# Statistics of the memory's second rows moved behind two weight subtractions, with multiplications of ones on TensorE

## The chip, the cores and the metric

The kernel runs on one core of one Trainium2 chip, and the metric is the device time of one execution in microseconds. A core has TensorE (PE, with its weight loads shown as PEld), VectorE (DVE), ScalarE (ACT), GpSimd (POOL) and SyncE (SP), each with its own queue of instructions in program order, and 16 DMA engines.

## The reference

It computes two blocks of two layers on 256 positions of width 1024, in float32; the first block's result is the second's input. The first block has an even layer (differential attention, a short gated convolution, cross attention to a memory of 256 rows) and an odd one (forgetting attention and cross attention); the second has a gated linear recurrence with a convolution, a pooling mixer, two more cross attentions and two feed-forward parts. What the change touches is the first thing the kernel computes, the memory's keys and values of the even layer, and a scalar of the attention:

```
def rms_norm(x, g):
    y = xf * lax.rsqrt(jnp.mean(xf * xf, axis=-1, keepdims=True) + EPS)
    return (y * g.astype(jnp.float32)).astype(x.dtype)

# in memory_cross_attention
mk, mv = jnp.split(rms_norm(mem, mem_g) @ w_mem_kv, 2, axis=-1)

# in differential_attention
lam = jnp.exp(jnp.sum(lp[0] * lp[1])) - jnp.exp(jnp.sum(lp[2] * lp[3])) + lam_init
```

## The kernel before

Every product of a weight matrix is computed in three passes of fp32r matmuls: a float32 operand is split into a rounded half `hi` and the rest `lo`, and hi·hi, hi·lo and lo·hi are added up in a PSUM bank (`passes`, L550 to L555). Weights come in units of 1 MB, each in two halves of 512 KB, through two slots of `w_raw`. For each half SyncE issues the load (`load`, L393), ScalarE writes `w_hi` (`hi`, L1272), VectorE writes `w_lo = w_raw - w_hi` (`lo`, L1928, the instruction at L1932), and TensorE multiplies. SyncE waits with the load of a half until the subtraction that last read its slot is done. Units 0 and 1 (`e_kv`) have their loads issued without a wait; units 2 and 3 (`e_kv` too) follow in the same slots.

At the start the memory has to be turned. TensorE transposes the 256 x 1024 rows in 16 transposes into banks 6, 7, 2 and 3 (`turn_pairs`, L674, recorded as L685), ScalarE writes `y_hi` with the gain as scale (`turned_hi`, L1400, L1408), and VectorE writes `y_lo` (`turned_lo`, L2051, L2059), pair by pair. The factor of the norm isn't applied to the rows: it is a factor of each row of the product, so ScalarE applies it when it copies the product out of the bank (`scaled_out`, L1341). The statistics behind it are VectorE's: `tile_stats` (L1954, two instructions of 512 columns a tile), `row_stats` (L1958: aggregation at L1966, two small operations, then a request to POOL by `ask`), and POOL computes the power -0.5 (`power`, L1843, L1846).

The order on every engine is written out by hand. VectorE's begins at L2382: statistics of both tiles of the memory, the request, then in two steps two pairs of `y_lo` and one weight subtraction each (`lo(0, 0, 1)` and `lo(0, 1, 2)`), then the subtractions of unit 1 (`lo(1, half, ...)`), the statistics of x's first 128 rows (L2394), a wait for lambda's parameters (L2395), two products and a reduction on them (L2397 to L2400), the subtractions of unit 2, the statistics of x's second rows (L2406), the request for them, the normalisation of x, and the subtractions of unit 3. POOL's begins at L1838: three memsets, among them of `ones`, a wait for the request named "mem" and its power (L1849), then the loads of the forget bias (L1850) and of lambda's parameters (L1851, 128 KB to 128 partitions), then the next powers. ScalarE's begins at L1648, and it waits for the power of "mem" before it goes on to unit 2.

TensorE's begins at L1039: a transpose of the memory's gains, a wait for both tiles of the memory, the 16 transposes, a transpose of the next gains (L1046), then `row_of("e_kv", 0)` and `1`, each 24 matmuls in two halves that wait for their subtractions (`lo_done`), two transposes of gain rows, and `row_of("e_kv", 2)`. Behind that the normalised rows of x are turned (`turn_pairs(nrm, 2)`, eight transposes), followed by the first half of `row_of("e_kv", 3)`, the other eight transposes, and its second half. Bank 0 belongs to `e_kv` unit 0, whose first matmul clears it.

The two places in which POOL and VectorE stand in line with the load of lambda:

```
            power("mem")
            pool.dma_start(bc[0:12, :], t["o_c_forget_b"].rearrange("a h -> h a")).then_inc(bc_in, 16)
            pool.dma_start(tp[:, 0:256], t["e_a_lambda"].rearrange("l a b -> l (a b)").to_broadcast([P, 256])).then_inc(lam_in, 16)
...
            v.wait_ge(x_in[0], 16)
            tile_stats(hv, 0)
            v.wait_ge(lam_in, 16)
```

Of the kernel before, what the change touches and what calls it, by code (L numbers as in the profile page):

```python
# [26 lines left out]
P = 128  # L27
# [118 lines left out]
GCOL = {}  # L146
# [35 lines left out]
def turned(name, groups=None):  # L182

    return TURN_AT[name] + (dict(TURNS)[name] if groups is None else groups)
# [25 lines left out]
def build_program(nc, t, out):  # L210

    with ExitStack() as ctx:
        def sb(name, words, dt=F32):
            return ctx.enter_context(nc.sbuf_tensor(name, [P, words], dt))

        def sem(name):
            return ctx.enter_context(nc.semaphore(name))
# [18 lines left out]
        ones = sb("ones", P)  # L236
# [3 lines left out]
        bank = [ctx.enter_context(nc.psum_tensor(f"bank{i}", [P, 512], F32)) for i in range(8)]  # L240
# [21 lines left out]
        def two(ap, w):  # L262
            return ap.rearrange("p (m w) -> p m w", w=w)

        def tv(ap):
            return ap.rearrange("p (k n) -> p k n", n=SEQ)

        hv = two(h[:, :], D)
        uh, ul, yh_, yl_ = tv(u_hi), tv(u_lo), tv(y_hi[:, :]), tv(y_lo[:, :])
        nrm = two(att[:, 0:2 * D], D)  # L270
# [78 lines left out]
        mem_in, id_in = [sem("mem_in0"), sem("mem_in1")], sem("id_in")  # L349
# [4 lines left out]
        init_done = sem("init_done")  # L354
        pow_asked, pow_done = sem("pow_asked"), sem("pow_done")
        dve_step, act_step, pool_step = sem("dve_step"), sem("act_step"), sem("pool_step")
        gains_t, gains_ready = sem("gains_t"), sem("gains_ready")
# [191 lines left out]
        def _(pe):  # L549
            def passes(out_ap, pairs, start, stop_, last=False):  # L550

                (ah, al), (bh, bl) = pairs
                pe.matmul(out_ap, ah, bh, start=start, stop=False, skip_group_check=True)  # L553
                pe.matmul(out_ap, ah, bl, start=False, stop=False, skip_group_check=True)  # L554
                return pe.matmul(out_ap, al, bh, start=False, stop=stop_, skip_group_check=True)  # L555

            def keep_busy(bk, n):

                for _ in range(n):
                    pe.matmul(bank[bk][:, 0:SEQ], ident, cst[:, C_TRI:C_TRI + SEQ], start=True, stop=True)  # L560

            def k8_unit(slot, bk, xh, xl, wait_lo, wait_bank, fresh=None, between=None):

                for half in range(2):
                    if fresh is not None:
                        pe.wait_ge(tL, fresh[half])
                    if half == 1 and between is not None:
                        between()  # L570
                    pe.wait_ge(lo_done, wait_lo + half)
                    if half == 0 and wait_bank is not None:
                        pe.wait_ge(evacuated, wait_bank)
                    for m in range(2):
                        for k in range(4 * half, 4 * half + 4):
                            a = 2048 * slot + SEQ * k + P * m
                            mm = passes(bank[bk][:, SEQ * m:SEQ * m + SEQ],
                                        ((w_hi[:, a:a + P], w_lo[:, a:a + P]), (xh[:, k, :], xl[:, k, :])),
                                        half == 0 and m == 0 and k == 0, k == 7)
                    mm.then_inc(half_done, 1)  # L580
# [22 lines left out]
            def row_of(name, j, xh, xl, fresh=None, between=None):  # L603

                u, kb = UNIT0[name] + j, BANK0[name] + j - j % 2
                first = j - j % 2
                row_unit(u % 2, j % 2, (unit_bank(name, first), unit_bank(name, first + 1)), xh, xl, 2 * u + 1,
                         kb - 1 if kb else None, fresh, between)
# [14 lines left out]
            def k8_phase(name, xh, xl, n=None, skip=0):  # L623
                base, kb = UNIT0[name] + skip, BANK0[name] + skip
                n = COUNT[name] if n is None else n
                if n == 2:
                    for j in range(2):
                        k8_unit((base + j) % 2, (kb + j) % 2, xh, xl, 2 * (base + j) + 1, kb + j - 1)
                    return
                with pe.Fori(0, n // 2) as i:  # L630
                    for j in range(2):
                        k8_unit((base + j) % 2, (kb + j) % 2, xh, xl, 4 * i + (2 * (base + j) + 1), 2 * i + (kb + j - 1))
# [81 lines left out]
            def beside_norm(phase, name, xh, xl):  # L714

                for j in range(2):
                    u, kb = UNIT0[phase] + j, BANK0[phase] + j
                    k8_unit(u % 2, unit_bank(phase, j), xh, xl, 2 * u + 1, kb - 1,
                            between=(lambda: turn_normed(name, 0)) if j == 1 else None)
                turn_normed(name, 1)  # L720
# [318 lines left out]
            pe.wait_ge(id_in, 16)  # L1039
            pe.wait_ge(mrow_in, 16)  # L1040
            pe.transpose(bank[5][:, 0:8], rows[0:8, 0:P], ident[0:8, 0:8]).then_inc(gains_t, 1)
            for m in range(2):
                pe.wait_ge(mem_in[m], 16)
            turn_pairs(nrm, 4, (6, 7, 2, 3))
            pe.wait_ge(rows_in, 16)
            pe.transpose(bank[4][:, 0:8], rows[32:40, 0:P], ident[32:40, 32:40]).then_inc(gains_t, 1)  # L1046
            for j in range(2):
                row_of("e_kv", j, yh_, yl_, fresh=(turned("mem", 2 * j + 1), turned("mem", 2 * j + 2)))
            pe.wait_ge(rows2_in, 16 * 21)
# [171 lines left out]
            for layer in range(2):  # L1221

                if layer == 1:
# [5 lines left out]
                    for c in range(8):  # L1229
# [3 lines left out]
                                  start=True, stop=False, skip_group_check=True)  # L1233
                        mm = pe.matmul(b[:, at + P:at + SEQ], hv[:, 1, P * c:P * c + P], PM[:, c // 2, SEQ:384],
                                       start=False, stop=True, skip_group_check=True)
# [4 lines left out]
                    for m in range(2):  # L1240
                        for g in range(4):
                            o = bank[DOWN[2 * m + g // 2]][:, SEQ * (g % 2):SEQ * (g % 2) + SEQ]
                            for k in range(2):
                                mm = pe.matmul(o, PT_[:, 2 * g + k, P * m:P * m + P], PW[:, 2 * g + k, :],
                                               start=(k == 0), stop=(k == 1))
# [18 lines left out]
        def _(act):  # L1264
# [263 lines left out]
            def attention(name):  # L1528
                lo, hi_ = PASS[name]
                for s in range(lo, hi_ + LAG):  # L1530
# [8 lines left out]
                    kind, j = beside(name, s)  # L1539
                    u = beside_unit(name, s)  # L1540
                    phase, before, _, _ = BESIDE[name]
                    if kind is None:
                        exponentials()
# [368 lines left out]
        def _(v):  # L1912
            steps = [0]

            def mark(ins):

                ins.then_inc(dve_step, 1)
                steps[0] += 1
# [9 lines left out]
            def lo(slot, half, ready):  # L1928

                v.wait_ge(hi_done, ready)  # L1930
                at = 2048 * slot + 1024 * half
                v.tensor_tensor(w_lo[:, at:at + 1024], w_raw[:, at:at + 1024],  # L1932
                                w_hi[:, at:at + 1024].bitcast(F32), ALU.subtract).then_inc(lo_done, 1)
# [20 lines left out]
            def tile_stats(src, m):  # L1954
                for j in range(2):
                    mark(v.bn_stats(bn6[:, 12 * m + 6 * j:12 * m + 6 * j + 6], src[:, m, 512 * j:512 * j + 512]))

            def row_stats(src, name, started=False):  # L1958

                at, _ = POW_AT[name]  # L1960
                if not started:
                    for m in range(2):
                        tile_stats(src, m)
                wait_own()
                for m in range(2):
                    mark(v.bn_aggr(mv[:, m, :], bn6[:, 12 * m:12 * m + 12]))  # L1966
                wait_own()
                o = pow_in[:, at:at + 2]
                mark(v.tensor_tensor(o, mv[:, :, 0], mv[:, :, 0], ALU.mult))
                wait_own()  # L1970
                mark(v.scalar_tensor_tensor(o, o, float(EPS), mv[:, :, 1], ALU.add, ALU.add))
                ask(name)
# [78 lines left out]
            def turned_lo(dh, dl, g, count, banks=(6, 7)):  # L2051

                for _ in range(count):
                    n = lo_n[0]
                    lo_n[0] += 1
                    v.wait_ge(tV, n + 1)
                    for j in range(2):
                        k = 2 * (n % 4) + j
                        ins = v.scalar_tensor_tensor(dl[:, k, :], bank[banks[n % len(banks)]][:, SEQ * j:SEQ * j + SEQ],  # L2059
                                                     gT[:, g + k:g + k + 1], dh[:, k, :].bitcast(F32),  # L2060
                                                     ALU.mult, ALU.subtract)
                    ins.then_inc(tL, 1)
# [317 lines left out]


            v.wait_ge(init_done, 3)  # L2382
            for m in range(2):
                v.wait_ge(mem_in[m], 16)
                tile_stats(nrm, m)
            row_stats(nrm, "mem", True)
            v.wait_ge(gains_ready, 1)
            for half in range(2):
                turned_lo(yh_, yl_, GCOL["e_mem_norm_g"], 2, (6, 7, 2, 3))
                lo(0, half, half + 1)  # L2390
            for half in range(2):
                lo(1, half, half + 3)
            v.wait_ge(x_in[0], 16)
# [433 lines left out]
```

## Time and profile before

| | us |
|---|---|
| median of 3 runs | 1300.85 |
| the three runs | 1300.65, 1300.85, 1302.69 |
| the profiled execution, its own time | 1302.49 |
| its span, first to last instruction | 1300.7 |
| busy in the span: TensorE / VectorE / ScalarE / POOL | 1268.6 / 894.6 / 688.9 / 62.3 |

The time lines give the start and length of an instruction, or of several alike that follow one another, and in brackets the idle time of the engine before it with what ended it. Matmuls overlap, so their spacing, not their length, is what one costs. The clock of a stretch is the one granted to TensorE as a share of 2.4 GHz. Times inside the profile count from the first instruction of the span.

### The profile page before, as it was taken

How to read it: one execution, taken by the hardware profiler on the slowest of the kernel's cores; microseconds unless marked ns; L12 is line 12 of the kernel's file. 1: busy time of each engine (PE TensorE's matmuls, PEld its weight loads, DVE VectorE, ACT ScalarE, POOL GpSimd, SP SyncE). 2: the span in 40 equal slices, each digit the busy share in tenths (PEclk: the TensorE clock that was granted, in tenths of full speed). 3: DMA queues.
4: the chain of work that ended last, by engine and by line, in shares of the span. 5: the costliest groups of instructions: out<-in, count | busy, mean ns of one | idle time of the engine just before them, and what ended most of it. 6: DMA issues, size and time to landing. Idle time of an engine off the chain costs nothing.

```text
span 1300.7 us, 19663 instructions
## 1 busy us (share of the span) xinstructions
PE 1268.6 (98%) x7244; PEld 1099.7 (85%) x7244; DVE 894.6 (69%) x1284; ACT 688.9 (53%) x1096; POOL 62.3 (5%) x71
## 2 busy tenths in 40 slices
PE   7999999999999999999999999999999999999997
PEld 6888899888788888898878988888887897888886
DVE  7667776775875655789896747666668646666667
ACT  6555778454567676457344544544444353444442
POOL 1012011000100000000000000000000000000000
PEclk9999999999999999999999999999999999999999
DMA  7666444556454445655355444767664443576662
GB/s 272 209 183 192 132 126 118 184 167 210 151 181 125 130 117 175 197 159 174 117 161 180 151 158 143 214 217 223 200 190 144 157 153 97 165 224 192 183 190 81
DMA packets 141544, 219.34 MB, mean 169 GB/s; under 512 B 6816, under 2 KB 95215, under 8 KB 141471
## 3 DMA queue, kind: packets, MB, share of 16 engines
q1 hardware_dynamic: 138206, 206.70, 51.2%
q0 software_dynamic: 2960, 10.93, 2.7%
q8 instruction: 47, 0.77, 0.2%
q10 hardware_dynamic: 304, 0.73, 0.1%
q14 instruction: 27, 0.21, 0.1%
HBM read 217.28 MB, written 1.05 MB: 168 GB/s over the span
## 4 chain that ended last, share of the span: by engine, by line
PE 82%; DVE 11%; ACT 4%; issue 2%; DMA 0%; POOL 0%; DVEq 0%; SPq 0%; ACTq 0%
PE bank L553 18%; PE bank L555 17%; PE bank L554 17%; PE bank L921 12%; PE bank L923 6%; DVE w_lo L1932 3%; DVE h L2089 1%; DVE small L2096 1%; PE bank L794 1%; PE bank L823 1%; PE bank L810 1%; ACT w_hi L1279 1%; DVE att L2577 1%; DVE att L1997 1%; PE bank L949 1%
## 5 line engine op out<-in xcount | busy, mean ns | idle before, releaser
L1932 DVE TENSOR_TENSOR w_lo<-w_raw,w_hi 128x1024 fp32r<-128x1024 f32 x388 | 472.1, 1223 | 251.4 <-ACT w_hi L1279 244.7
L1279 ACT ACTIVATE w_hi<-w_raw 128x1024 fp32r<-128x1024 f32 x388 | 408.9, 1059 | 397.6 <-PE bank L555 320.9
L921 PE MATMUL bank<-u_s,w_hi 128*128 128x512 f32 x672 | 238.2, 399 | 0.4 <-DVE u_s L2071 0.4
L553 PE MATMUL bank<-w_hi,y_hi 128*128 128x512 f32 x528 | 210.6, 399 | 6.7 <-DVE w_lo L1932 3.9
L555 PE MATMUL bank<-w_hi,y_lo 128*128 128x512 f32 x528 | 206.8, 392 | 0.0
L554 PE MATMUL bank<-w_lo,y_hi 128*128 128x512 f32 x528 | 206.4, 391 | 0.0
L923 PE MATMUL bank<-u_s,w_lo 128*128 128x256 f32 x672 | 188.7, 281 | 0.0
L553 PE MATMUL bank<-u_s,w_hi 128*128 128x256 f32 x544 | 156.6, 288 | 2.6 <-DVE u_s L2071 2.6
L555 PE MATMUL bank<-u_s,w_lo 128*128 128x256 f32 x544 | 153.9, 283 | 0.0
L554 PE MATMUL bank<-u_s,w_hi 128*128 128x256 f32 x544 | 153.8, 283 | 0.0
L921 PEld LDWEIGHTS bank<-u_s,w_hi 128*128 128x128 f32 x672 | 126.3, 188 | 32.0 <-DVE u_s L2071 0.8
L553 PE MATMUL bank<-w_hi,u_s 128*128 128x512 f32 x336 | 133.0, 396 | 0.8 <-ACT nat L1338 0.7
L555 PE MATMUL bank<-w_hi,u_s 128*128 128x512 f32 x336 | 131.0, 390 | 0.0
L554 PE MATMUL bank<-w_lo,u_s 128*128 128x512 f32 x336 | 130.8, 389 | 0.0
L923 PEld LDWEIGHTS bank<-u_s,w_lo 128*128 128x128 f32 x672 | 126.9, 189 | 0.7
L553 PEld LDWEIGHTS bank<-w_hi,y_hi 128*128 128x128 f32 x528 | 99.6, 189 | 30.5 <-DVE w_lo L1932 4.0
L555 PEld LDWEIGHTS bank<-w_hi,y_lo 128*128 128x128 f32 x528 | 99.4, 188 | 21.7
L554 PEld LDWEIGHTS bank<-w_lo,y_hi 128*128 128x128 f32 x528 | 99.6, 189 | 19.5
L553 PEld LDWEIGHTS bank<-u_s,w_hi 128*128 128x128 f32 x544 | 104.2, 192 | 3.7 <-DVE u_s L2071 3.4
L554 PEld LDWEIGHTS bank<-u_s,w_hi 128*128 128x128 f32 x544 | 104.3, 192 | 0.1
L555 PEld LDWEIGHTS bank<-u_s,w_lo 128*128 128x128 f32 x544 | 104.2, 191 | 0.0
L1846 POOL TENSOR_TENSOR pow_out<-pow_in,mhalf 128x1 f32<-128x1 f32 (+5 forms) x27 | 38.7, 1433 | 787.3 <-DVEq L1926 787.3
(302 smaller groups left out, 1615.4 us busy)
## 6 DMA issues: line engine op xcount, KB each, us to landing
w_raw<-in_e_w_in SPq DMA_DIRECT2D x56, 512.0 KB, 3.8
w_raw<-in_o_w_in SPq DMA_DIRECT2D x56, 512.0 KB, 3.8
w_raw<-in_ffn_wg SPq DMA_DIRECT2D x44, 512.0 KB, 4.1
w_raw<-in_ffn_wu SPq DMA_DIRECT2D x44, 512.0 KB, 4.4
w_raw<-in_ffn_wd SPq DMA_DIRECT2D x44, 512.0 KB, 3.6
w_raw<-in_ab_w_in SPq DMA_DIRECT2D x24, 512.0 KB, 3.9
w_raw<-in_e_w_out SPq DMA_DIRECT2D x16, 512.0 KB, 3.6
w_raw<-in_o_w_out SPq DMA_DIRECT2D x16, 512.0 KB, 3.6
```

What stands on the lines that cost most here:

```text
L553: pe.matmul(out_ap, ah, bh, start=start, stop=False, skip_group_check=True)
L554: pe.matmul(out_ap, ah, bl, start=False, stop=False, skip_group_check=True)
L555: return pe.matmul(out_ap, al, bh, start=False, stop=stop_, skip_group_check=True)
L794: mm = pe.matmul(bank[SC[pr]][:, SEQ * m:SEQ * m + SEQ], XQT[:, 2 * hd + j, P * m:P * m + P], (KT2 if g < 32 else KT1)[:, 2 * hd + j, :], ...
L810: mm = pe.transpose(bank[PTB][:, dst:dst + P], s[:, src:src + P], ident)
L823: mm = pe.matmul(o[:, SEQ * j:SEQ * j + SEQ], V2[:, k, cs], p[:, SEQ * k:SEQ * k + SEQ], start=(k == 0), stop=(k == 1))
L921: pe.matmul(two(bank[banks[m]][:, :], SEQ), w_hi[:, a:a + P], u_both[:, :, SEQ * k:SEQ * k + SEQ], start=(k == 0), stop=False, skip_group_ ...
L923: mm = pe.matmul(bank[banks[m]][:, 0:SEQ], w_lo[:, a:a + P], uh[:, k, :], start=False, stop=(k == 7), skip_group_check=True)
L949: pe.matmul(o[:, :, ts], w_hi[:, a:a + P], u_both[:, :, SEQ * k + P * tile:SEQ * k + P * tile + P], start=(k == 0 and tile == 0), stop=Fal ...
L1279: act.activation(w_hi[:, at:at + 1024], w_raw[:, at:at + 1024], ACT.Copy).then_inc(hi_done, 1)
L1846: pool.tensor_tensor(pow_out[:, at:at + w], pow_in[:, at:at + w], mhalf[:, 0:w], ALU.pow)\
L1932: v.tensor_tensor(w_lo[:, at:at + 1024], w_raw[:, at:at + 1024], w_hi[:, at:at + 1024].bitcast(F32), ALU.subtract).then_inc(lo_done, 1)
```

## The change

TensorE multiplies the 128 x 128 tile of ones by itself into bank 0, seven times between the first transpose and its wait for the memory, and twice behind the transpose of the next gains. VectorE computes the statistics of the memory's first rows as before, then the `y_lo` pairs and the two subtractions of unit 0, and only then the statistics of the second rows, the aggregation and the request to POOL; the subtractions of unit 1 follow.

```
+            def warm(n):
+                for _ in range(n):
+                    pe.matmul(bank[0][:, 0:P], ones[:, :], ones[:, :], start=True, stop=True)
...
             pe.transpose(bank[5][:, 0:8], rows[0:8, 0:P], ident[0:8, 0:8]).then_inc(gains_t, 1)
+            pe.wait_ge(init_done, 3)
+            warm(7)
             for m in range(2):
                 pe.wait_ge(mem_in[m], 16)
             turn_pairs(nrm, 4, (6, 7, 2, 3))
             pe.wait_ge(rows_in, 16)
             pe.transpose(bank[4][:, 0:8], rows[32:40, 0:P], ident[32:40, 32:40]).then_inc(gains_t, 1)
+            warm(2)
...
             v.wait_ge(init_done, 3)
-            for m in range(2):
-                v.wait_ge(mem_in[m], 16)
-                tile_stats(nrm, m)
+            v.wait_ge(mem_in[0], 16)
+            tile_stats(nrm, 0)
+            v.wait_ge(gains_ready, 1)
+            turned_lo(yh_, yl_, GCOL["e_mem_norm_g"], 2, (6, 7, 2, 3))
+            lo(0, 0, 1)
+            turned_lo(yh_, yl_, GCOL["e_mem_norm_g"], 2, (6, 7, 2, 3))
+            lo(0, 1, 2)
+            v.wait_ge(mem_in[1], 16)
+            tile_stats(nrm, 1)
             row_stats(nrm, "mem", True)
-            v.wait_ge(gains_ready, 1)
-            for half in range(2):
-                turned_lo(yh_, yl_, GCOL["e_mem_norm_g"], 2, (6, 7, 2, 3))
-                lo(0, half, half + 1)
             for half in range(2):
                 lo(1, half, half + 3)
```

## Rows read from the trace of the kernel before

**Rows 1.** The page: span, and engines on the chain that ended last.

```profile
span 1300.7 us, 19663 instructions
...
PE 82%; DVE 11%; ACT 4%; issue 2%; DMA 0%; POOL 0%; DVEq 0%; SPq 0%; ACTq 0%
```

**Rows 2.** Stretches: length; busy PE, PEld, DVE, ACT, POOL; clock; DMA share; GB/s.

```profile
6.31:9.80 3.49, 3.49 (x17) 3.23 (x17) 3.12 (x10) 2.30 (x5) 1.40 (x3) 1.00 1.04 376
...
12.60:16.00 3.40, 3.40 (x10) 2.63 (x9) 3.40 (x4) 3.40 (x6) 0.00 (x0) 0.50 0.77 212
...
16.00:24.11 8.11, 8.11 (x37) 6.61 (x36) 6.29 (x14) 3.19 (x5) 0.00 (x0) 1.00 0.95 317
```

**Rows 3.** Time line, TensorE (start us, us, engine, line, operation, tiles, count, idle before).

```profile
6.31 3.33 PE L685 MATMUL bank<-cst,att 128*128 128x128 f32 x16 [3.24 <-DMA att<-in_mem]
...
9.11 0.53 PE L685 MATMUL bank<-cst,att 128*128 128x128 f32 x3
...
11.47 0.47 PE L553 MATMUL bank<-w_hi,y_hi 128*128 128x512 f32 x1 [1.68 <-DVE w_lo L1932]
...
16.60 0.39 PE L553 MATMUL bank<-w_hi,y_hi 128*128 128x512 f32 x1
...
23.42 0.39 PE L553 MATMUL bank<-w_hi,y_hi 128*128 128x512 f32 x1
...
24.20 0.48 PE L553 MATMUL bank<-w_hi,y_hi 128*128 128x512 f32 x1
...
29.75 1.03 PE L685 MATMUL bank<-cst,att 128*128 128x128 f32 x8
```

**Rows 4.** Time line, TensorE at full clock: f32 matmuls of 128 columns.

```profile
400.86 0.39 PE L781 MATMUL bank<-att 128*128 128x128 f32 x2
...
401.08 0.60 PE L782 MATMUL bank<-att 128*128 128x256 f32 x2
```

**Rows 5.** Time line, ScalarE: the memory's first halves y_hi.

```profile
7.50 1.63 ACT L1408 ACTIVATE y_hi<-bank,gT 128x256 fp32r<-128x256 f32 x4 [4.21 <-PE bank L685]
```

**Rows 6.** Time line, VectorE.

```profile
7.52 0.28 DVE L1966 BATCH_NORM_AGGREGATE small<-small 128x2 f32<-128x12 f32 x2
...
8.46 1.66 DVE L2059 SCALAR_TENSOR_TENSOR y_lo<-bank,gT,y_hi 128x256 fp32r<-128x256 f32 x4 [0.27 <-ACT y_hi L1408]
...
10.10 1.23 DVE L1932 TENSOR_TENSOR w_lo<-w_raw,w_hi 128x1024 fp32r<-128x1024 f32 x1
...
12.82 3.48 DVE L1932 TENSOR_TENSOR w_lo<-w_raw,w_hi 128x1024 fp32r<-128x1024 f32 x3
...
16.22 1.28 DVE L1956 BATCH_NORM_STATS2 small<-h 128x6 f32<-128x512 f32 x2
...
17.41 0.20 DVE L2397 TENSOR_TENSOR att<-att 128x64 f32<-128x64 f32 x1
...
19.18 1.23 DVE L1932 TENSOR_TENSOR w_lo<-w_raw,w_hi 128x1024 fp32r<-128x1024 f32 x1 [1.10 <-ACT w_hi L1279]
...
22.04 1.28 DVE L1956 BATCH_NORM_STATS2 small<-h 128x6 f32<-128x512 f32 x2
...
26.26 2.35 DVE L1932 TENSOR_TENSOR w_lo<-w_raw,w_hi 128x1024 fp32r<-128x1024 f32 x2
```

**Rows 7.** Time line, POOL: the first power and the issue of lambda's load.

```profile
8.40 0.71 POOL L1846 TENSOR_TENSOR pow_out<-pow_in,mhalf 128x2 f32<-128x2 f32 x1 [7.16 <-DVEq L1926]
...
9.73 0.60 POOL L1851 DMA_DIRECT2D att<-in_e_a_lambda  x1
```

**Rows 8.** DMA issues of POOL (queue, KB, median us from issue to landing).

```profile
att<-in_e_a_lambda POOLq DMA_DIRECT2D x1, 128.0 KB, 6.2
...
bc<-in_o_c_forget_b POOLq DMA_DIRECT2D x1, 0.0 KB, 6.4
...
att<-in_o_w_in POOLq DMA_DIRECT2D x1, 48.0 KB, 4.9
...
nat<-in_mem_ln_g POOLq DMA_DIRECT2D x1, 512.0 KB, 3.8
```

## The prediction

> **What bounds the kernel now.** I read the page, then the stretches of the start, then the time line of each engine, then the transfers. The page [rows 1] gives a span of 1300.7 us with TensorE on 82% of the chain that ended last. After the start it hardly rests, so a time gained or lost there reaches the end only as it moves the moment from which TensorE runs on. I follow one such moment: the first matmul of e_kv unit 2 at 24.20 [rows 3].
>
> The start has two rests of TensorE. It waits 3.24 us for the memory's second rows, turns both tiles in 16 transposes from 6.31 to 9.6, and rests from 9.80 to 11.47, 1.67 us, until the first weight subtraction is done [rows 3]. From 12.60 to 16.00 its granted clock is 0.50, that is 1.2 GHz; afterwards it is 1.00, 2.4 GHz [rows 2]. The row of 6.31 to 9.80 prints 1.00 too [rows 2], but the 16 transposes in it take 3.33 us (0.21 each), while the last three, from 9.11, take 0.53 in all and eight at 29.75 take 1.03, spaced about 0.11 [rows 3]. They ran at 1.2 GHz until about 9.2. The stretch at 0.50 costs half of its 3.40 us, 1.7.
>
> The profiled execution took 1302.49 us against a median of 1300.85 (1300.65 to 1302.69). The 1.64 between them is the price of that stretch; I read the two lower runs as runs without it. By the rows, unit 2 would start at about 22.6 in those.
>
> **Part by part: the ones.** Where TensorE runs fast, two f32 matmuls of 128 columns start 0.22 apart [rows 4]; at half clock that is 0.44, and seven take 3.1. They start where TensorE's rest begins, at 3.07 (6.31 less 3.24 of idle time), and end at 6.2, before the memory's transposes at 6.31: they cost nothing, and 0.1 to 0.3 if they run over. If they bring the clock up, the first four transposes end at 6.9, not 7.4, and ScalarE starts at 7.01 instead of 7.50 [rows 5]. The two ones behind the transposes cost 0.44 in a rest. But the transposes now end near 8.4 instead of 9.80, so TensorE rests from 8.8 to its first matmul at 11.0: 2.2 us, longer than the 1.67 after which the clock fell before. The ones do not close the second rest.
>
> On the transposes the Trainium skill (TensorE: Matmul & The Clock Gate, Part 4) says that the full clock does not engage in transpose mode. The spacing in this trace, from 0.21 to 0.11 during transposes alone, speaks against it; by that rule the first four would still end at 7.4 and nothing would be gained at the start.
>
> **The moved statistics.** On VectorE y_lo follows ScalarE's start by 0.96 [rows 5, 6], so it may start at 7.97. In the old order the statistics and the aggregation held VectorE until 8.19 (8.46 less 0.27 of idle time), so part of the ones' gain needs this move. The new order, each step by the distance of starts in [rows 6]: four y_lo 1.64, first subtraction at 9.61, TensorE 1.37 behind it (11.47 less 10.10) at 10.98; second subtraction 2.72 later at 12.33; 1.13 for it (3.48 for three, less overlap); second-row statistics from 13.46, 1.28 long, aggregation at 14.78; POOL's power 0.88 behind that (8.40 less 7.52) [rows 6, 7] at 15.66, where it was 8.40; third subtraction 0.06 before that, once the request is out, at 15.60; TensorE may use it at 16.97. Before it started near 13.95.
>
> TensorE needs 0.227 a matmul (30 in the 6.82 from 16.60 to 23.42) [rows 3], so 24 of unit 0 with 0.09 for the first take it from 10.98 to 16.53. It waits 0.44 for the third subtraction, runs unit 1 to 22.5 and would begin unit 2 at 22.6. That is 1.6 before the profiled 24.20 and nothing before the runs without the slow stretch: the 0.49 won at the start is spent at the third subtraction.
>
> **What is queued behind the moved request.** POOL stands at its first power until the aggregation asks for it, and issues the loads of the forget bias and of lambda only behind it: lambda 1.33 after the power's start (9.73 less 8.40) [rows 7], now at 16.99 instead of 9.73. VectorE waits for lambda behind the statistics of x's first rows. It had it in time: the first product ran at 17.41 without a wait [rows 6]. Now it is through those statistics at 16.73 + 1.13 + 1.19 = 19.05, and lambda's 128 KB took 6.2 us to land [rows 8]: 23.2. Behind it come 0.8 for three small operations and the signal, then the subtraction of unit 2's first half and TensorE 1.37 behind its start, so unit 2 starts 2.2 after the landing. In the old order that subtraction began at 19.18 [rows 6].
>
> The landing is what I can't read. Nearest is the same transfer, 6.2; the nearest other small one of POOL took 4.9 and one of 512 KB 3.8 [rows 8]. They put unit 2 at 25.4, 24.1 and 23.0. It still shares the queues with weight loads, as it did then, which favours 6.2, but the short loads of gain rows that went out around it then are done by 17. I take 5.4: landing 22.4, unit 2 at 24.6, 0.4 after 24.20. Down the road, the third weight unit's subtraction began 4.22 after the statistics of x's second rows [rows 6]; they now start at 25.5, so the subtraction at 29.7, usable at 31.1, while TensorE has finished unit 2 (5.55, from 24.20 to 29.75) and eight transposes 0.11 apart at 24.6 + 5.55 + 0.88 = 31.0: 0.1 more.
>
> The Trainium skill (DMA: Bandwidth & Descriptors, Anatomy of one DMA, SWDGE path) gives a POOL-issued DMA some 2.0 us plus its bytes at 436 GB/s. By it, an estimate of 2.3 us, lambda lands at 19.3 and the wait is almost nothing; the same transfer's 6.2 in this trace is far from it.
>
> **Sum.** Against the profiled execution's own time: 1302.49 + 0.4 + 0.1 = **1303.0 us**, 2.15 above the median. In it a slow stretch behind the rest at 8.8 to 11.0 costs nothing: it ends unit 1 near 23.8 instead of 22.5, both before 24.6. About 0.2% (2.6 us) is what a measurement of this kernel can tell from no change.
>
> **Rivals.**
> - *Late lambda and a slow clock behind it (slower).* Lambda takes its old 6.2 us, and TensorE, having run units 0 and 1 fast, rests from 22.5 to 25.4 and falls to 1.2 GHz as it did after 1.67. Unit 2 at 25.4 gives 1303.9; the slow stretch adds up to 1.7, less what lies in the rest: 1304.5 to 1305.5. It decides from a landing 5.9 us after the issue, which is where the bound of 0.2% lies without a slow clock. For it: the only row of this transfer. Against: its company in the queue differs.
> - *Lambda is there in time.* It lands within about 3.8 us: 1302.49 - 1.2 = 1301.3, or 1300.9 with no wait, unit 2 at 22.6. For it: POOL's other loads; the page's rule gives this too. Against: 6.2, and 6.4 for the forget bias, of hardly any bytes [rows 8].
> - *The ones don't lift the clock in time,* or run over. Everything above moves back 0.5: 1303.6.
> - *Faster by the bound.* Only if the runs of before mostly have the slow stretch, and after none and no wait.
>
> **How the numbers follow.** Forecast 0.42, late lambda 0.28, lambda in time 0.18, clock not lifted 0.08, faster 0.04. The forecast lies 0.45 under the bound of "slower" and gives a third of its chance to it; late lambda two thirds, since the median of before may itself lie higher in the comparison; clock not lifted half: slower 0.36, faster 0.04, same 0.60. The range goes from lambda in time, 1300.6, to most of late lambda, 1305.0.
>
> **What would show it.** Right: POOL's first power near 15.7 and lambda's issue near 17; a wait of VectorE on the DMA of lambda before L2397, 2 to 4 us; TensorE's first e_kv matmul near 11.0, a wait of 0.4 near 16.5, unit 2 from 23.7 to 25.4. Wrong: L2397 at 19.1 with no wait (then 1300.9), transposes still 0.21 apart at 6.3, or a rest of TensorE after 26.

## The result, and the profile after

The changed kernel took 1304.50 us (median of 15 runs, 1302.99 to 1305.61) beside 1301.99 (15 runs, 1300.19 to 1303.22) for the kernel before: a ratio of 1.0021, 95% interval 1.0013 to 1.0028. It is slower, clear of the noise; whether by more than the 0.2% that the prediction named as its bound, the interval leaves open. Its profiled execution took 1305.61, 3.12 more than that of before. It is the slowest of the fifteen, 1.11 above their median, so what the profile shows of the loss need not be there in full in the others.

The page of the changed kernel, its span and the engines on its chain, beside [rows 1]:

```profile
span 1303.8 us, 19699 instructions
...
PE 81%; DVE 11%; ACT 4%; issue 2%; DMA 1%; POOL 0%; DVEq 0%; ACTq 0%; POOLq 0%
```

The shares tell as little as before, but the 1% for DMA on the chain is new. Time line of TensorE, changed kernel, beside [rows 3]. One product of the ones leaves two records, so 14 are seven of them and 4 are two:

```profile
2.92 3.35 PE L565 MATMUL bank<-ones 128*128 128x128 f32 x14
6.37 3.06 PE L690 MATMUL bank<-cst,att 128*128 128x128 f32 x16
...
9.52 0.71 PE L565 MATMUL bank<-ones 128*128 128x128 f32 x4
11.54 0.47 PE L553 MATMUL bank<-w_hi,y_hi 128*128 128x512 f32 x1 [1.31 <-DVE w_lo L1940]
...
17.52 0.47 PE L553 MATMUL bank<-w_hi,y_hi 128*128 128x512 f32 x1 [0.23 <-DVE w_lo L1940]
...
25.79 0.80 PE L553 MATMUL bank<-w_hi,y_hi 128*128 128x512 f32 x1 [2.39 <-DVE w_lo L1940]
26.39 0.63 PE L554 MATMUL bank<-w_lo,y_hi 128*128 128x512 f32 x1
26.81 0.63 PE L555 MATMUL bank<-w_hi,y_lo 128*128 128x512 f32 x1
...
29.29 0.40 PE L555 MATMUL bank<-w_hi,y_lo 128*128 128x512 f32 x1
29.52 0.40 PE L553 MATMUL bank<-w_hi,y_hi 128*128 128x512 f32 x1
...
32.95 1.04 PE L690 MATMUL bank<-cst,att 128*128 128x128 f32 x8
```

Unit 2 starts at 25.79, where it started at 24.20. Its first matmuls are 0.43 apart and the later ones 0.23; the turn of x behind it starts 7.16 after it, and 5.55 before [rows 3]. So 1.59 us come from the later start and 1.61 from a slow clock behind the rest of 2.39; together 3.20, and the profiled times differ by 3.12. e_nat is the product behind e_kv; its first matmul starts at 36.98 before and at 40.20 after. The profiled time less that start is 1265.51 before and 1265.41 after: nothing is lost later. Stretches of the changed kernel (columns as in [rows 2]):

```profile
11.54:17.52 5.98, 5.75 (x24) 4.41 (x25) 5.72 (x13) 4.91 (x9) 1.31 (x1) 1.00 0.85 275
...
25.76:29.17 3.41, 3.38 (x8) 2.71 (x9) 2.92 (x7) 0.98 (x8) 0.25 (x1) 0.50 0.61 169
29.17:40.20 11.03, 11.03 (x58) 9.25 (x57) 9.36 (x14) 5.85 (x11) 0.48 (x1) 1.00 0.65 218
```

The slow stretch of 12.60 to 16.00 [rows 2] has gone from unit 0 (clock 1.00 there, matmuls 0.23 apart) and stands in unit 2 instead, where no rest swallows it. Time line of VectorE, changed kernel, beside [rows 6]:

```profile
5.06 1.29 DVE L1964 BATCH_NORM_STATS2 small<-att 128x6 f32<-128x512 f32 x2 [5.06 <-DMA att<-in_mem]
8.50 1.66 DVE L2067 SCALAR_TENSOR_TENSOR y_lo<-bank,gT,y_hi 128x256 fp32r<-128x256 f32 x4 [2.16 <-ACT y_hi L1416]
10.17 1.23 DVE L1940 TENSOR_TENSOR w_lo<-w_raw,w_hi 128x1024 fp32r<-128x1024 f32 x1
...
14.01 1.28 DVE L1964 BATCH_NORM_STATS2 small<-att 128x6 f32<-128x512 f32 x2
15.33 0.28 DVE L1974 BATCH_NORM_AGGREGATE small<-small 128x2 f32<-128x12 f32 x2
...
16.15 2.36 DVE L1940 TENSOR_TENSOR w_lo<-w_raw,w_hi 128x1024 fp32r<-128x1024 f32 x2 [0.15 <-DVE pow_in L1979]
18.43 1.28 DVE L1964 BATCH_NORM_STATS2 small<-h 128x6 f32<-128x512 f32 x2
23.69 0.23 DVE L2407 TENSOR_TENSOR att<-att 128x64 f32<-128x64 f32 x1 [3.98 <-DMA att<-in_e_a_lambda]
```

Freeing VectorE early won nothing in this execution: it waits 2.16 for y_hi, and y_lo starts at 8.50 (8.46 before), because the transposes run at 1.2 GHz again until about 8.7, read from their spacing as in the prediction. The statistics of the second rows are done at 15.3. Behind them VectorE makes two subtractions and the statistics of x's first rows, and then it waits 3.98 us for lambda. Why lambda is late shows on POOL, changed kernel, beside [rows 7]:

```profile
16.21 1.74 POOL L1854 TENSOR_TENSOR pow_out<-pow_in,mhalf 128x2 f32<-128x2 f32 x1 [14.96 <-DVEq L1934]
17.89 0.69 POOL L1858 DMA_DIRECT2D bc<-in_o_c_forget_b  x1
18.57 0.60 POOL L1859 DMA_DIRECT2D att<-in_e_a_lambda  x1
```

and in the DMA issues, changed kernel, beside [rows 8]:

```profile
att<-in_e_a_lambda POOLq DMA_DIRECT2D x1, 128.0 KB, 5.1
```

The issue has gone from 9.73 to 18.57; it lands at 23.67. The power is 1.74 long, not 0.71, which no step of mine had.

### The profile page after: what moved, and what is told of

It reads as the page before. It is cut to its first block, busy times and chain, and to the rows that moved or that the text cites. A ratio compares the mean times of both kernels' runs of the same rounds, so it can differ in the third digit from the quotient of the medians.

```text
span 1303.8 us, 19699 instructions
## 1 busy us (share of the span) xinstructions
PE 1272.7 (98%) x7262; PEld 1103.0 (85%) x7262; DVE 894.6 (69%) x1284; ACT 689.3 (53%) x1096; POOL 63.4 (5%) x71
## 4 chain that ended last, share of the span: by engine, by line
PE 81%; DVE 11%; ACT 4%; issue 2%; DMA 1%; POOL 0%; DVEq 0%; ACTq 0%; POOLq 0%
PE bank L553 17%; PE bank L555 17%; PE bank L554 17%; PE bank L926 12%; PE bank L928 6%; DVE w_lo L1940 3%; DVE h L2097 1%; DVE small L2104 1%; PE bank L799 1%; PE bank L828 1%; PE bank L815 1%; ACT w_hi L1287 1%; DVE att L2587 1%; DVE att L2005 1%; PE bank L954 1%
```

## The experiments

My theory after this result: the loss is lambda's lateness alone (the request moved behind two subtractions, POOL standing at the power, the load queued behind it) and the slow clock that the wait brings; the ones and the freed VectorE would give a little if lambda came in time. The rivals: the second-row statistics in front of unit 1 cost time themselves, or the ones do. All experiments are edits of the changed kernel, except e4_before_late_lambda, which is one of the kernel before; each is timed beside the kernel before, whose median was 1302.35 both beside e1 to e4 (27 runs) and beside e5 to e8 (33 runs). This table gathers what the sections below read, from the profiled executions: own time (us), start of unit 2, and the distance from there to the first matmul of e_nat. It is one execution of each.

| kernel | own time | unit 2 | to e_nat |
|---|---|---|---|
| before | 1302.49 | 24.20 | 12.78 |
| after | 1305.61 | 25.79 | 14.41 |
| e1_lambda_first | 1301.58 | 23.41 | 12.78 |
| e2_ones_only | 1302.56 | 24.25 | 12.81 |
| e3_move_only | 1304.11 | 25.15 | 13.59 |
| e4_before_late_lambda | 1306.64 | 26.72 | 14.42 |
| e5_lambda_tenth_us | 1301.01 | 23.30 | 12.82 |
| e6_stats_behind_unit1 | 1300.00 | 22.52 | 12.80 |
| e7_more_ones | 1300.03 | 22.08 | 12.77 |
| e8_third_waits_power | 1302.67 | 23.82 | 13.60 |

The own time less the start of e_nat's first matmul is 1264.7 to 1265.5 in all ten.

### Lambda's load taken out from behind the power (e1_lambda_first)

```
-            power("mem")
             pool.dma_start(bc[0:12, :], ...)
             pool.dma_start(tp[:, 0:256], t["e_a_lambda"]...)
+            power("mem")
```

> The changed kernel, with POOL's two loads (forget bias, lambda) issued ahead of the power of mem instead of behind it; nothing else moves. Theory (late lambda): lambda's load goes out near 1.5 us instead of 18.57, VectorE's 3.98 us of waiting before L2407 is gone, TensorE's rest of 2.39 before e_kv unit 2 is gone and unit 2 starts near 23.2 instead of 25.79; with no rest there the clock doesn't fall at 25.8. Time 2.6 us under the changed kernel, or 4.2 where that one has the slow stretch: near 1300.9, ratio to before 0.999. 128 KB more in front of the memory's rows may cost 0.3. Rival (the moved statistics themselves, through the later third subtraction and all that VectorE does behind it): the time stays within 0.5 of the changed kernel's 1304.5, unit 2 still starts after 25. Rival (the ones cost TensorE time): 1304 or more as well.

1302.71 us (11 runs, 1301.04 to 1305.20), ratio to the kernel before 1.0007, 0.9998 to 1.0016. Lambda is issued at 2.22 and lands at 9.57; VectorE and TensorE wait for it no more, unit 2 starts at 23.41, and no slow stretch follows. In its profile the loss is gone; over its runs most of it, 1.8 of 2.5 us. The theory's 1300.9 was missed by 1.8 all the same, and the runs spread over 4 us. The loads now go out among the first weights: the first weight half lands at 9.26 instead of 8.16. In the profiled execution that costs 0.20 (first subtraction at 10.37, 10.17 in the changed kernel). Why the runs spread so is not shown.

### Held back until the tenth microsecond (e5_lambda_tenth_us)

```
-            power("mem")
+            pool.wait_ge(hi_done, 1)
             pool.dma_start(bc[0:12, :], ...)
             pool.dma_start(tp[:, 0:256], t["e_a_lambda"]...)
+            power("mem")
```

> The changed kernel with POOL's two loads ahead of the power of mem, as in e1_lambda_first, but held until ScalarE has written the first w_hi (hi_done 1, near 10.1 us), so that they go out when they did in the kernel before and not in front of the first weights. In e1 lambda at 2.22 put the first weight's landing at 9.26 instead of 8.16. Theory (lambda's lateness was the loss, its early load the rest of e1's): lambda lands near 16 to 17, no wait of VectorE, first e_kv matmul 11.5, a rest of 0.2 to 0.6 at the third subtraction, unit 2 near 23.0 to 23.2; time 1301.2, in runs with a stretch at 1.2 GHz at most 0.7 more; ratio to before 0.9985 to 0.9998, and 2.5 to 3.5 us under the changed kernel. Rival (the moved statistics cost besides lambda): ratio 1.0005 or more.

1301.01 us (11 runs, 1300.06 to 1302.35), ratio 0.9993, 0.9983 to 1.0002. Issued at 11.57, close to its old moment, lambda takes 6.5 us and lands at 18.07, before VectorE asks for it. This is the changed kernel with all of its parts and without late lambda: some 3.5 us faster than the changed kernel by the medians, and by its interval not slower than the kernel before by more than 0.02%. TensorE still rests 0.28 before unit 1, for the third subtraction.

### Late lambda alone, in the kernel before (e4_before_late_lambda)

```
             power("mem")
+            pool.wait_ge(half_done, 3)
             pool.dma_start(bc[0:12, :], ...)
             pool.dma_start(tp[:, 0:256], t["e_a_lambda"]...)
```

> The kernel before, with one wait added on POOL between the power of mem and the two loads: until TensorE is done with the first half of e_kv unit 1 (19.7 to 21.5 us). Statistics and ones as before. It delays lambda alone. Theory: lambda's issue near 21 to 22, landing near 26 to 27, unit 2 2.1 after the landing at 28 to 29, some 4.5 us after the profiled 24.20; the clock falls behind the rest of 4 to 6 us, another 1.0 to 1.5. Time 1306 to 1308, ratio 1.0035 to 1.005. Rival (lambda's wait isn't on the path, since POOL or VectorE has slack): 1302.

1307.43 us (5 runs, 1306.17 to 1307.59), ratio 1.0042, 1.0028 to 1.0056. The time line of its TensorE and VectorE:

```profile
26.72 0.59 PE L553 MATMUL bank<-w_hi,y_hi 128*128 128x512 f32 x1 [3.84 <-DVE w_lo L1933]
27.11 0.63 PE L554 MATMUL bank<-w_lo,y_hi 128*128 128x512 f32 x1
...
24.61 0.23 DVE L2398 TENSOR_TENSOR att<-att 128x64 f32<-128x64 f32 x1 [7.11 <-DMA att<-in_e_a_lambda]
```

With nothing changed but the issue's moment (20.97, landing 24.58), the same picture stands there as in the changed kernel: a rest, and matmuls 0.43 apart behind it. In both kernels with the slow clock in unit 2, it is 14.4 from there to e_nat, not 12.8. The later start, 2.52, and the longer way, 1.64, make up the 4.15 by which the profiled times differ.

### Each half of the change alone (e2_ones_only, e3_move_only)

The first keeps the ones and puts VectorE's old order back; the second keeps the move and leaves the ones out.

```
-            v.wait_ge(mem_in[0], 16)
-            tile_stats(nrm, 0)
+            for m in range(2):
+                v.wait_ge(mem_in[m], 16)
+                tile_stats(nrm, m)
+            row_stats(nrm, "mem", True)
             v.wait_ge(gains_ready, 1)
...
-            v.wait_ge(mem_in[1], 16)
-            tile_stats(nrm, 1)
-            row_stats(nrm, "mem", True)
```

```
-            pe.wait_ge(init_done, 3)
-            warm(7)
...
-            warm(2)
```

> The kernel before with the seven and the two multiplications of ones alone, statistics in their old place. Theory (late lambda is the loss, the ones only keep the clock up): lambda in time as before, first e_kv matmul near 11.5, no stretch at 1.2 GHz between 12 and 16 us, unit 2 near 22.6 to 22.8. Time about 1300.9 in most runs, ratio to before 0.9990 to 0.9997 (the runs of before lie at 1300.2 to 1303.2, some with that stretch). Rival (the ones are the loss): ratio 1.0015 or more. Rival (the ones don't keep the clock): ratio 1.000, the stretch is there.

> The changed kernel without the multiplications of ones: only the statistics are moved. Theory (late lambda): POOL's first power near 16.2, lambda lands near 23.7, unit 2 starts near 25.8 whether or not units 0 and 1 run partly at 1.2 GHz, since lambda is later than both. Time 1303.4 to 1304.9, ratio 1.0010 to 1.0025. Where the slow stretch lies at 12 to 16 us it is hidden, and the rest before unit 2 is shorter (1 to 2 us), so it falls a second time less often than in the changed kernel. Rival (the ones are the loss): ratio 1.000, 1302.

The ones alone: 1300.96 us (11 runs), ratio 0.9996, 0.9987 to 1.0005. The move alone: 1304.61 us (11 runs), ratio 1.0020, 1.0011 to 1.0029. The move carries the whole loss, the ones none of it. The profiled execution of the ones alone took 1302.56. Its time line, TensorE and VectorE:

```profile
6.50 1.94 PE L690 MATMUL bank<-cst,att 128*128 128x128 f32 x16 [0.45 <-DMA att<-in_mem]
...
11.55 0.47 PE L553 MATMUL bank<-w_hi,y_hi 128*128 128x512 f32 x1 [2.32 <-DVE w_lo L1940]
...
8.62 1.66 DVE L2067 SCALAR_TENSOR_TENSOR y_lo<-bank,gT,y_hi 128x256 fp32r<-128x256 f32 x4 [0.24 <-DVE pow_in L1979]
```

and a stretch of it (columns as in [rows 2]):

```profile
12.57:15.98 3.41, 3.41 (x10) 2.64 (x9) 3.41 (x5) 3.41 (x7) 0.00 (x0) 0.50 0.82 235
```

Here the ones did lift the clock: 16 transposes in 1.94 us. y_hi is there at 7.23, but VectorE is busy with statistics until 8.38, so nothing comes of it; the rest grows to 2.32 and the clock falls behind it all the same. That the ones need the move to bring the start forward, as the prediction had it, shows here. The forecast of no slow stretch failed in this execution. Seven of the eleven runs took 1300.66 to 1301.04 and four 1302.28 to 1302.67, so in most of them the stretch may be absent; there is no profile of one of the seven.

The move alone runs units 0 and 1 partly at the slow clock (matmuls 0.43 apart until 15.04), so TensorE has less to wait: a rest of only 0.69 before unit 2 (25.15) and no slow clock behind it. And yet it is 13.59 to e_nat. Its waits from 29 to 42 us (who waited for whom: us in all, times, the longest) name what is left:

```profile
PEld bank L690 <- DVE u_s L2064: 0.8, 2, 0.5
```

VectorE, late by lambda, comes to the normalised rows of x late, and runs three subtractions in one go (30.38 to 33.78) before it reads the turned rows out of the banks; TensorE's second turn has to wait for those banks, 0.8 us. The kernel before has no such wait. The prediction had 0.1 for all that lies down this road, and for another wait, that for unit 3's subtraction.

### The power beside a subtraction (e8_third_waits_power)

The 1.74 us of the power was the second thing to settle. In the changed kernel the third subtraction starts at 16.15 and ends at 17.38; the power starts at 16.21 and ends at 17.94, 0.56 after that end. The move alone repeats it:

```profile
16.15 1.73 POOL L1851 TENSOR_TENSOR pow_out<-pow_in,mhalf 128x2 f32<-128x2 f32 x1 [14.91 <-DVEq L1931]
...
16.10 2.36 DVE L1937 TENSOR_TENSOR w_lo<-w_raw,w_hi 128x1024 fp32r<-128x1024 f32 x2 [0.15 <-DVE pow_in L1976]
```

With lambda's load ahead of it (e5) the power starts 0.01 before the subtraction. The time line of POOL and VectorE of that kernel:

```profile
16.26 0.73 POOL L1854 TENSOR_TENSOR pow_out<-pow_in,mhalf 128x2 f32<-128x2 f32 x1 [4.09 <-DVEq L1935]
...
16.27 2.40 DVE L1941 TENSOR_TENSOR w_lo<-w_raw,w_hi 128x1024 fp32r<-128x1024 f32 x2
```

The kernel before had the long form too, two rows of its time line that I had not read:

```profile
276.54 1.79 POOL L1846 TENSOR_TENSOR pow_out<-pow_in,mhalf 128x2 f32<-128x2 f32 x1 [29.03 <-DVEq L1926]
...
276.53 1.22 DVE L1932 TENSOR_TENSOR w_lo<-w_raw,w_hi 128x1024 fp32r<-128x1024 f32 x1
```

So the theory: a power that starts behind a subtraction waits for its end. The rival: the power is just slow in that crowded moment. The test keeps the subtraction off:

```
             row_stats(nrm, "mem", True)
+            v.wait_ge(pow_done, 1)
             for half in range(2):
                 lo(1, half, half + 3)
```

> The changed kernel with one wait added: VectorE holds the third subtraction until POOL's power of mem is done. In the changed kernel the power took 1.73 us (16.21 to 17.94) where it took 0.71 before, and it ended 0.56 behind the end of the subtraction that started beside it (17.38). Theory (POOL's power stood still while VectorE subtracted, which made lambda 1.0 later): power of 0.55 to 0.75 from 16.2, lambda's issue near 17.5 instead of 18.57, VectorE's third subtraction 0.7 later (16.9), unit 2 about 0.7 to 1.0 earlier than 25.79, time 0.5 to 1.0 under the changed kernel: 1303.6. Rival (the power's length is chance or its own): power still over 1.4, time 0 to 0.7 over the changed kernel.

1302.89 us (11 runs, 1301.91 to 1303.42), ratio 1.0008, 0.9999 to 1.0017: 1.6 us less than the changed kernel with a wait added, where 0.5 to 1.0 was forecast. Its time line, POOL, TensorE and VectorE:

```profile
15.52 0.71 POOL L1854 TENSOR_TENSOR pow_out<-pow_in,mhalf 128x2 f32<-128x2 f32 x1 [14.28 <-DVEq L1934]
...
16.85 0.60 POOL L1859 DMA_DIRECT2D att<-in_e_a_lambda  x1
...
17.64 0.47 PE L553 MATMUL bank<-w_hi,y_hi 128*128 128x512 f32 x1 [1.03 <-DVE w_lo L1940]
...
23.82 0.50 PE L553 MATMUL bank<-w_hi,y_hi 128*128 128x512 f32 x1 [0.32 <-DVE w_lo L1940]
...
21.73 0.23 DVE L2408 TENSOR_TENSOR att<-att 128x64 f32<-128x64 f32 x1 [1.90 <-DMA att<-in_e_a_lambda]
```

The power is 0.71 and the issue 1.33 behind its start, as in the kernel before. In this profile it also starts 0.69 earlier, since the clock rose before the transposes here, which the added wait cannot have done: unit 2 begins 1.97 earlier than in the changed kernel, of which 1.03 is the power's length, 0.69 that earlier start and some 0.25 a shorter transfer (4.8 for 5.1). Lambda is still 1.90 late. Unit 2 starts 0.38 before that of the kernel before, and still the time is not better: the 0.8 at the second turn is back (13.60).

### The statistics behind unit 1, and more ones (e6_stats_behind_unit1, e7_more_ones)

With lambda's load free of the power, the second-row statistics need not stand before unit 1 at all. The first of the two is e5 with

```
             lo(0, 1, 2)
+            for half in range(2):
+                lo(1, half, half + 3)
             v.wait_ge(mem_in[1], 16)
             tile_stats(nrm, 1)
             row_stats(nrm, "mem", True)
-            for half in range(2):
-                lo(1, half, half + 3)
```

and the second adds ones before the first transpose and behind the sixteen:

```
+            pe.wait_ge(init_done, 3)
+            warm(3)
             pe.wait_ge(id_in, 16)
...
-            warm(2)
+            warm(8)
```

> e5 with the statistics of the second rows, the aggregation and the request one step further back, behind both subtractions of unit 1. Theory (the third subtraction's delay costs 0.2 to 0.6 of TensorE's rest, and no other reader of the power is early): third subtraction near 14.0 as in the kernel before, no rest of TensorE before unit 1, power near 18.4, ScalarE's first half of unit 2 1 us later than in e5 but still in time; unit 2 near 22.6 to 22.8 without a slow stretch, 24.2 with one, as in the kernel before. Time 1300.9 or 1302.5 by run, ratio 0.999 to 1.000. Rival (the power is now too late for ScalarE or for the order behind): unit 2 after 23.5 and ratio above 1.0005.

> e6 with three more multiplications of ones ahead of everything on TensorE (from 1.3 us, while it waits for the identity) and eight instead of two behind the gains' transpose, so that both rests are filled. Theory (the clock follows what TensorE did before; a lifted clock brings the first y_hi forward by 0.5 and the moved statistics let VectorE use it): transposes 0.11 apart from 6.4 on, ScalarE's first y_hi near 7.1, first e_kv matmul 11.0 to 11.1, no stretch at 1.2 GHz in the first 30 us, unit 2 near 22.2. Time 1300.4, ratio 0.998 to 0.999, and narrower than the kernel before. Rival (the rest can't be filled without running over, or the first weight's landing near 8.2 to 8.4 sets the start): first matmul 11.4 or later, ratio 0.9993 or more.

The first took 1300.44 us (11 runs, 1299.99 to 1302.63), ratio 0.9989, 0.9980 to 0.9998; the second 1300.25 (11 runs, 1299.82 to 1301.66), ratio 0.9986, 0.9977 to 0.9995. Both beat both kernels, by the medians about 2 us against the kernel before and 4 against the changed one; between them the runs don't decide. From the first e_kv matmul to unit 2 it is 11.14 in e6 and 11.64 in e5: the third subtraction's delay costs 0.5 once lambda is in time. The time line of TensorE in the second:

```profile
6.22 2.01 PE L690 MATMUL bank<-cst,att 128*128 128x128 f32 x16
...
8.32 2.05 PE L565 MATMUL bank<-ones 128*128 128x128 f32 x16
10.95 0.47 PE L553 MATMUL bank<-w_hi,y_hi 128*128 128x512 f32 x1 [0.57 <-DVE w_lo L1943]
...
16.54 0.39 PE L553 MATMUL bank<-w_hi,y_hi 128*128 128x512 f32 x1
```

The rest before unit 0 is 0.57, there is none before unit 1, and unit 2 starts at 22.08. Of its 11 runs 10 lie below 1300.5, of the 33 of the kernel before beside it 4 (its lowest 1300.15): by the runs, the gain is mostly that a time which the kernel before reaches now and then has become the rule.

## Why the prediction was right or wrong

**The range held, the likeliest case did not come.** 1304.5 lies 1.5 above the 1303.0 and within 1300.6 to 1305.0. What came in the profiled execution is the outcome of the rival "late lambda and a slow clock behind it" (1304.5 to 1305.5, chance 0.28; its own sum for unit 2 at 25.4 gives 1303.8, not 1303.9): a rest of TensorE of 2.39 and a slow stretch behind it. It did not come by the rival's condition, a transfer of 6.2 us; that took 5.1, and the issue was later. How many of the fifteen runs had the slow stretch is not shown. With e3's 0.81 longer way in place of the 1.61, an estimate from these profiles, the changed kernel without it would take 1302.49 + 1.59 + 0.81 = 1304.9, so late lambda alone can account for a median of 1304.50. "Same" at 0.60 leaned on a forecast only 0.45 below the bound, while two of its terms, the shortest power and a clock that rises in time, could err upwards alone.

**Part of the nearness is luck.** The forecast lies 2.15 above the median of three runs, and the measured difference of the medians is 2.51. But 1.64 of the 2.15 is how far the profiled execution of before lay above that median; the effect that the prediction worked out was only 0.5, and profile against profile it was 3.12.

**What bounds the kernel** was right: one moment, the start of unit 2, carried the difference, and all behind e_nat kept its time. So was the order of events on POOL and VectorE, and who waits for whom.

**The ones lift the clock: not in this profile.** The forecast had the transposes at full clock, y_hi at 7.01 and the first matmul at 10.98; measured 7.56 and 11.54. That moved everything back by 0.55 (power 16.21 for 15.66), the size I gave to the rival "clock not lifted", which I had priced as an alternative and not as something that adds to late lambda. Its chance of 0.08 was too low: of the six profiled kernels with seven ones two had the clock up in time (16 transposes in 1.94, e2 and e8), the others took 2.37 (e1), 2.52 (e6), 2.98 (e5) and 3.06. In e8 it came as forecast, y_hi at 6.93 and the first matmul at 10.85. On the transposes the traces stay against the Trainium skill (TensorE: Matmul & The Clock Gate, Part 4), which says that the full clock does not engage in transpose mode: 16 took 1.94 us in two kernels and 3.33 in [rows 3].

**The ones don't close the second rest** was right (1.31 here, 2.32 alone). That the clock falls behind it was wrong for the changed kernel, where it held at 1.00, and right for the ones alone.

**Lambda's issue 1.33 after the power's start: the term that failed in the sum.** It was 2.36, since the power took 1.74 beside VectorE's subtraction. I took 0.71 from the one row of [rows 7], where VectorE had no subtraction at hand, though my own step placed the third subtraction 0.06 before the power. With the 0.55 from the clock, the issue came at 18.57 instead of 16.99. These two, 1.03 and 0.55, less 0.3 for a shorter transfer and 0.1 behind the landing, are the 1.19 by which unit 2 came later than the 24.6 forecast.

**The landing.** The latency, which I called the thing I can't read, was 5.1 against my 5.4: it took 0.3 off. Landing 23.67 for 22.4, unit 2 at 25.79 for 24.6, 2.1 behind the landing (2.2 worked out); the wait of VectorE, forecast at 2 to 4, was 3.98. The rival's point of decision, 5.9 us behind an issue at 16.99, is a landing at 22.9. A transfer of only 5.1 passed that point, because the issue had moved: the landing was the thing to bound, not the latency.

The Trainium skill's fit (DMA: Bandwidth & Descriptors, Anatomy of one DMA) would have made it 2.3 us, an estimate; no execution here came near, the shortest is 3.6.

**The slow clock: the largest term that the forecast put at nothing.** I placed it where it is hidden, behind the second rest; it came behind the rest before unit 2, which the forecast itself had (from 22.5 to 24.6), and cost 1.61. The sum with measured terms is 1302.49 + 1.59 + 1.61 = 1305.69 against 1305.61.

**The 0.1 down the road** was too little for executions without the slow clock: 0.8 at the second turn (e3, e8), where TensorE waits for banks and not for the subtraction that I had followed. With the slow clock this wait is gone: the profile of the changed kernel shows none.

**The third subtraction**, 16.15 for 15.60, made TensorE wait 0.23 (0.44 forecast), which the wait for lambda hides here.

## What to carry to other kernels

When a step is moved, list what stands behind it on every queue that it feeds, and move loads with a due time of their own out from behind it: here the whole loss was one 128 KB load that nobody had meant to move, and the change without it (e5) is not measurably slower. Price an instruction from rows in which its neighbours are those it will have, and ask of each rival whether it adds to the others. An early issue is not free either: at 2.2 us the same load pushed the first weights' landing back by 1.1.

## What the runs showed of the hardware

**GpSimd's power and VectorE's subtraction: one of them holds the other up.** Where the subtraction started 0.05 ahead, the power took 1.74 (after: 16.15, 16.21) and 1.73 (e3: 16.10, 16.15), and ended 0.56 behind the subtraction's end. Where the power started 0.01 ahead it took 0.73 (e5: 16.26, 16.27) and 0.72 (e1: 16.34, 16.35), and the two subtractions 2.40 instead of 2.36. At a tie the printed starts don't tell who was first. The power for the row statistics between 274 and 281 us starts level with a subtraction or 0.01 behind it in all ten profiles; it took 1.79 or 1.80 beside a subtraction of 1.22 or 1.23 in nine of them, and in e5 it took 0.71 beside one of 1.27:

```profile
275.69 0.71 POOL L1854 TENSOR_TENSOR pow_out<-pow_in,mhalf 128x2 f32<-128x2 f32 x1 [29.03 <-DVEq L1935]
...
275.68 1.27 DVE L1941 TENSOR_TENSOR w_lo<-w_raw,w_hi 128x1024 fp32r<-128x1024 f32 x1
```

The Trainium skill (SBUF — State Buffer, SBUF: two separate sides) says that a VectorE instruction with two inputs in SBUF contends with a GpSimd instruction that reads SBUF, and that whichever starts first holds the port pair for the whole instruction. With the subtraction first, the 1.74 agrees. It doesn't fit the other order: a power of 0.73 in front held the subtraction up by about 0.04, not by its length.

**The clock after a rest.** It fell behind rests of 1.67 (before), 2.32 (e2), 2.39 (after) and 3.84 (e4), and was up behind 1.31 (after), 1.36 (e5), 1.37 (e4), 1.79 (e6), 1.91 (e8) and 2.16 (e1). The length of the rest alone doesn't tell; what else decides was not settled. Nor does what TensorE did before, as far as these kernels show. e3 and e4 begin alike: 16 transposes in 3.64 and 3.65, all at the slow spacing, and a rest of 1.31 and 1.37. Behind it e3's matmuls are 0.43 apart until 15.04 (the clock column prints 1.00 there, as it does for the first transposes of [rows 2]), and e4's are 0.23 apart. The time line of TensorE, e3 first:

```profile
11.48 0.77 PE L553 MATMUL bank<-w_hi,y_hi 128*128 128x512 f32 x1 [1.31 <-DVE w_lo L1937]
12.05 0.63 PE L554 MATMUL bank<-w_lo,y_hi 128*128 128x512 f32 x1
...
11.48 0.47 PE L553 MATMUL bank<-w_hi,y_hi 128*128 128x512 f32 x1 [1.37 <-DVE w_lo L1933]
11.79 0.40 PE L554 MATMUL bank<-w_lo,y_hi 128*128 128x512 f32 x1
```

In the same way the same seven ones before the same transposes gave 1.94 to 3.06 us for the sixteen. No run here shows why.

**One transfer, many latencies.** Lambda's 128 KB took 3.6 (e4), 4.5 (e3), 4.8 (e8), 5.1 (after), 5.6 (e7), 6.2 (before), 6.3 (e2), 6.5 (e5), 6.8 (e6) and 7.4 us (e1): longest when issued first, at 2.22 among the first weight loads, shortest when issued last, at 20.97.
